# One decoder layer on Trainium2: the low parts of the expert stage's weights, three quarters on GpSimd and one quarter on VectorE, or all on GpSimd

## The reference

```python
qry = (xb @ p['peer_wq']).reshape(PEER_BLOCK, PEER_HEADS, 2, PEER_HALF)
...
top_s, pos = lax.top_k(cand, PEER_TOPK)          # 8 heads x 16 experts a token
idx = jnp.take_along_axis(cidx, pos, axis=-1)
gates = jax.nn.softmax(top_s, axis=-1)
u_rows = p['peer_u'][idx]
act = jax.nn.gelu(jnp.einsum('phkd,pd->phk', u_rows, xb))
coef = gates * act
return jnp.einsum('phk,phkd->pd', coef, p['peer_v'][idx])
```

## Time and profile before

| | us |
|---|---|
| median of 3 runs | 4422.45 |
| the profiled execution, its own time | 4424.48 |
| its span on the core | 4422.7 |
| PE busy in the span | 3754.4 (85%) |
| DVE busy | 3025.6 (68%) |
| POOL busy | 2101.4 (48%) |
| ACT busy | 1477.9 (33%) |
| turns of the expert stage | 2249 to 4399 |

### The profile page before, as it was taken

How to read it: one execution, slowest core, us unless ns; L and a number is a source line. 1 busy time by engine, 2 the same in 40 slices (tenths; PEclk the granted TensorE clock), 3 DMA queues, 4 the chain that set the end, 5 groups by cost and what they waited for, 6 DMA issues and landing times. The chain is left out here.

```text
span 4422.7 us, 65816 instructions
## 1 busy us (share of the span) xinstructions
PE 3754.4 (85%) x24298; PEld 3491.1 (79%) x24298; DVE 3025.6 (68%) x4531; ACT 1477.9 (33%) x1891; POOL 2101.4 (48%) x1162
## 2 busy tenths in 40 slices
PE   6777999999996898987678989988888888888887
PEld 3337888898885797987578988888888888888886
DVE  5777644555554213897967877776778888888886
ACT  5664343443442113223333333232222222222222
POOL 2432222212224133324356767666666667676672
PEclk9998999999997898998889999999999999999998
DMA  8981212222212122223389999999999999999994
GB/s 308 358 314 64 78 64 82 77 77 73 75 67 68 60 98 108 81 70 111 137 315 386 402 395 408 393 384 366 364 381 380 386 401 387 390 395 392 408 403 157
DMA packets 253130, 1090.63 MB, mean 247 GB/s; under 512 B 25352, under 2 KB 78856, under 8 KB 172296
## 3 DMA queue, kind: packets, MB, share of 16 engines
q1 hardware_dynamic: 167440, 543.60, 32.9%
q0 software_dynamic: 73728, 536.90, 29.9%
q10 hardware_dynamic: 11776, 7.52, 0.5%
HBM read 1047.54 MB, written 40.40 MB: 246 GB/s over the span
## 5 line engine op out<-in xcount | busy, mean ns | idle before, releaser
L248 POOL TENSOR_TENSOR wlo<-raw,whi 128x1024 fp32r<-128x1024 f32 x551 | 1343.1, 2441 | 1495.4 <-ACT whi L244 1487.6
L244 ACT CAST whi<-raw 128x1024 fp32r<-128x1024 f32 x672 | 698.8, 1049 | 1284.7 <-DMA raw<-in_u 535.5
L263 PE MATMUL gps<-hi_d,whi 128*128 128x320 f32 x2048 | 661.6, 323 | 168.3 <-POOL wlo L248 116.1
L2096 PE MATMUL gps<-chi,whi 128*128 128x320 f32 x2048 | 653.8, 319 | 124.7 <-DVE outacc L2225 82.0
L263 PE MATMUL gps<-lo_d,whi 128*128 128x320 f32 x2048 | 651.7, 318 | 0.0
L263 PE MATMUL gps<-hi_d,wlo 128*128 128x320 f32 x2048 | 650.6, 318 | 0.0
L2096 PE MATMUL gps<-clo,whi 128*128 128x320 f32 x2048 | 643.2, 314 | 0.0
L2096 PE MATMUL gps<-chi,wlo 128*128 128x320 f32 x2048 | 643.1, 314 | 0.0
L2183 DVE SCALAR_TENSOR_TENSOR dps<-ring,coef,dps 128x2048 f32<-128x2048 f32 x252 | 591.8, 2348 | 7.6 <-DMA ring<-in_v_rows,spi 3.1
L2170 DVE CUSTOM_DVE_ANT_0 ring<-ring,dps 128x2048 f32<-128x2048 f32 x256 | 582.2, 2279 | 0.0
L263 PEld LDWEIGHTS gps<-hi_d,whi 128*128 128x128 f32 x2048 | 402.1, 196 | 186.7 <-POOL wlo L248 126.4
(11 more groups left out here) (388 smaller groups left out, 6064.6 us busy)
## 6 DMA issues: line engine op xcount, KB each, us to landing
raw<-in_u SPq DMA_DIRECT2D x256, 512.0 KB
raw<-in_v SPq DMA_DIRECT2D x256, 512.0 KB
wada<-in_w_ada SPq DMA_DIRECT2D x96, 1024.0 KB, 6.4
raw<-in_w_in SPq DMA_DIRECT2D x96, 512.0 KB
gateD<-gst SPq DMA_DIRECT2D x8, 2560.0 KB, 7.5
gate<-gateD SPq DMA_DIRECT2D x32, 640.0 KB
raw<-in_w_out SPq DMA_DIRECT2D x32, 512.0 KB
raw<-in_w_q SPq DMA_DIRECT2D x32, 512.0 KB
```

The lines of the kernel that those rows point to most:

```text
L244: act.copy(whi[:, k.slot, :], raw_of(k)).then_inc(W.hi, 1)
L248: pool.tensor_tensor(wlo[:, k.slot, :], raw_of(k), whi[:, k.slot, :].bitcast(F32), ALU.subtract).then_inc(W.lo, 1)
L263: m = pe.matmul(gps[:, bank, 0:DT], w, x[:, kt, :], start=(kt == 0 and n == 0), stop=(kt == KT - 1 and n == 2))
L2096: m = pe.matmul(gps[:, 2 + dt, 0:DT], w[:, slot, cols], x[:, buf, c, :], start=(c == 0 and n == 0), stop=(c == NG - 1 and n == 2))
```

## The change

`by_dve` and `split_lo_dve` go, and with them the semaphore `w_lo_dve`. GpSimd makes the low part of every half, in the order of the halves; the 123 that VectorE made are put into GpSimd's stream at their place. Waits for a low part (TensorE's before a half, SyncE's before the load four halves later) are all on one semaphore that counts up by one for each half. Nothing is changed in what TensorE, ScalarE and SyncE do, or in the order in which they do it.

```diff
--- before.py
+++ after.py
@@ -188,7 +188,6 @@
 
         W = Sems()
         W.loaded0, W.loaded1, W.hi, W.lo, W.used = sems(stack, "w_loaded0", "w_loaded1", "w_hi", "w_lo", "w_used")
-        W.lo_dve, = sems(stack, "w_lo_dve")
         w_row = sems(stack, *(f"w_row{n}" for n in range(RING)))
         W.act_steps, W.dve_steps = sems(stack, "w_act_steps", "w_dve_steps")
         act_total, dve_total = [0], [0]
@@ -200,18 +199,9 @@
         N_SHARED = 2 + 12 * H + 2 * KT + 4 * H + 18
         N_DEEP = N_SHARED - 2
 
-        def by_dve(k):
-
-            return k.c >= N_SHARED - 1 and k.slot == 3
-
         def lo_done(k):
 
-            m = k.c - N_SHARED
-            if by_dve(k):
-                return W.lo_dve, m // 4 + 2 + k.i * (k.per // 4)
-            if m < -4 or m < 0 and isinstance(k.n, int):
-                return W.lo, k.n + 1
-            return W.lo, N_SHARED + m // 4 * 3 + m % 4 + 1 + k.i * (k.per // 4 * 3)
+            return W.lo, k.n + 1
 
         def deep(k):
 
@@ -247,11 +237,6 @@
             pool.wait_ge(W.hi, k.n + 1)
             pool.tensor_tensor(wlo[:, k.slot, :], raw_of(k), whi[:, k.slot, :].bitcast(F32),
                                ALU.subtract).then_inc(W.lo, 1)
-
-        def split_lo_dve(dve, k):
-            dve.wait_ge(W.hi, k.n + 1)
-            dve.tensor_tensor(wlo[:, k.slot, :], raw_of(k), whi[:, k.slot, :].bitcast(F32),
-                              ALU.subtract).then_inc(W.lo_dve, 1)
 
         def gemm_dense(pe, k, half, bank):
 
@@ -2035,8 +2020,7 @@
                             fetched[0] += 1
 
                     def lo(k):
-                        if not by_dve(k):
-                            split_lo(pool, k)
+                        split_lo(pool, k)
 
                     def A(g, buf, k, after):
                         for c in range(NG):
@@ -2152,7 +2136,6 @@
                         dve.engine_nop().then_inc(S.acc, 1)
                     for n in range(EARLY * NG):
                         dve.engine_nop().then_inc(S.gel, 1)
-                    dve.engine_nop().then_inc(W.lo_dve, 1)
                     ch = Chain(dve, W.dve_steps, dve_total)
                     taken = [0]
 
@@ -2197,10 +2180,6 @@
                         dve.tensor_tensor(clo[:, buf, c, :], gel, chi[:, buf, c, :].bitcast(F32),
                                           ALU.subtract).then_inc(S.clo, 1)
 
-                    def lo(k):
-                        if by_dve(k):
-                            split_lo_dve(dve, k)
-
                     def A(g, buf, k, after):
                         for c in range(NG):
                             due = rows_due((g - 2) // 2, g % 2 * NG + c)
@@ -2210,8 +2189,6 @@
                             gated(g, c, gps[:, c % 2, 0:DT])
                             take()
                             rest(g, buf, c, gps[:, c % 2, 0:DT])
-                            for j in (2 * c + 2, 2 * c + 3):
-                                lo(k.plus(j) if j < 8 else after.plus(j - 8))
 
                     def B(g, buf, k, after):
                         dve.wait_ge(S.acc, g * KT + 2)
@@ -2223,11 +2200,6 @@
                                     dve.wait_ge(W.used, k.plus(s).n + 1)
                                 out = outacc[:, 2 * s + dt, :]
                                 dve.tensor_tensor(out, out, gps[:, 2 + dt, 0:DT], ALU.add).then_inc(S.acc, 1)
-                                if dt == 0:
-                                    if s < 6:
-                                        lo(k.plus(s + 2))
-                                    elif after is not None:
-                                        lo(after.plus(s - 6))
                             take()
                             if after is None:
                                 if s % 4 == 0:
```

## The result

The kernel became slower. Medians of four runs each on the same chip: 4424.51 us before (4420.88 to 4432.38) and 4476.85 us after (4475.20 to 4490.93), a ratio of 1.0116 (95%: 1.0092 to 1.0139). The forecast was 4400 us with a range up to 4450 us. The profiled execution of the changed kernel took 4490.93 us, 14 us above its median; some of its excess is that run's own, such as the 10 us by which its turns begin later (2259 us, before 2249).

The account below looks back on a forecast made before the run. The prediction took the DMA engines, bringing in gathered rows and weight halves, to bound the expert stage. Its terms, -15 - 5 + 1 - 5 = -24 us on 4424.5 us, gave 4400 us, range 4355 to 4450 us.

Parts of the forecast that it names:

- What bounds the kernel: Expert stage: DMA share 0.98 of 1.02 in both long stretches, so any quicker engine can win at most 76 us.
- VectorE loses 123 low parts: Expert stage: some 190 us leave VectorE; TensorE's removable stalls are 104 us, 31 while u is gathered, 73 while v is.
- How much of that reaches the end: Turns gathering u and v: 5 of 31 and 10 of 73 us are gained, -15 us, bounds 0 and -76.
- The last two Bs: End of the stage, without gathers: TensorE's 3.98 us stop for VectorE's low part goes; -5 us, bounds 0 and -8.
- The first turn: 2249 to 2385 us, DMA not yet full throughout: SyncE no longer waits for VectorE's late part; -5 us, bounds 0 and -6.
- GpSimd's added work: GpSimd gains 123 low parts, 299 us, and is busy 83% and 81% in the long stretches; it keeps up, 0 us.
- Two SBUF readers: Last B: two moved low parts may each stop a small VectorE addition for up to 2 us; +1 us, at most +4.
- DMA alone: Rival: the DMA sets the pace, stalls removed return as load waits, only the end gains; 4419 us, chance 0.22.
- stalls paid in full: Rival: TensorE's removed stalls all count, since earlier high parts start earlier loads and DMA idle patches close; 4342 us, chance 0.08.
- GpSimd becomes the bound: Rival: in As, GpSimd's added parts delay its backlog and later loads; 4453 us, with As of u 4492 us, chance 0.23.
- The signs: Profile after: no TensorE stall for VectorE's low parts, bank waits 78 to 26 us, longer load waits, DMA share 0.98 to 1.0.

Follow-up runs that it names:

- The gates' edit: Gates loaded from ScalarE's queue, one B earlier, instead of SyncE's: kernel before 4345.46 us (0.9807), changed kernel 4338.68 us (0.9798).
- The short parts: Changed kernel, with each of the 123 low parts added to GpSimd covering 128 of 1024 columns: 4484.51 us, 1.0129.
- the edits that moved the lead: Changed kernel, gathers of u issued two rows later: 4441.96 us; also each B's last gather behind the next A's third-half low part: 4421.38 us.
- the idle operations in A and B: Changed kernel, with 123 operations that change nothing where VectorE's low parts stood: 4406.47 us; only those in Bs 4439.08 us, only those in As 4463.66 us.

## Why the prediction was wrong, step by step

- *What bounds the kernel*: right and too coarse. The DMA share of 0.98 was read as "the DMA can't be sped up by more than 76 us", but not as "it can fall". It fell to 0.94. The gates' edit shows that even the ceiling was too low: it made the kernel before 1.9% faster, 88 us on the same chip. The share of 0.98 says how long packets kept the engines, not what they moved: the same rows show 387 and 394 GB/s where the undisturbed stretch had 425, which by the same sum leaves 156 us instead of 76. With the gates moved, the two stretches run at 402 to 414 GB/s.
- *VectorE loses 123 low parts*: right. Waits for them 52 to 0 us, banks 78 to 38 us (26 expected).
- **The step that failed is "How much of that reaches the end"**, with its bounds of 0 and -76 us. I took the worst case as "all given back at the next load". TensorE gave back more than it won: per A of u 5.0 us lost for 2.0 won. The bound of 0 rested on the thought that what the loads wait for is only the full DMA. It is also what stands ahead of them in the queue and among the gathers, and the moment of issue. Both hang on when GpSimd gathers and makes its low parts, and VectorE set that by freeing buffers late (`S.taken`). I had even noted that at an A "everybody waits for the loads queued behind the gates", and used it only to make the gain small.
- *The last two Bs*, -5 us: wrong, -0.3. VectorE's low part ahead of the bank went, and TensorE's stop there went from 3.98 to 2.99 us only. VectorE now stood at a gathered row that had come 0.77 us late:

```profile
4384.70 2.35 DVE L2166 SCALAR_TENSOR_TENSOR ring<-ring,coef,dps 128x2048 f32<-128x2048 f32 x1 [0.77 <-DMA ring<-in_v_rows,spi]
4386.96 0.48 DVE L2180 TENSOR_TENSOR clo<-gps,chi 128x320 fp32r<-128x320 f32 x1
4387.36 0.87 DVE L2202 TENSOR_TENSOR outacc<-outacc,gps 128x320 f32<-128x320 f32 x2
```

  The same row had stood there before (4316.70 us, 2.34 us), ahead of the low part; I had counted the low part as the whole stop.
- *The first turn*, -5 us: wrong. It took 140 us instead of 136, by the same stall (16.6 us of waits for GpSimd's low parts instead of 11.6).
- *GpSimd's added work*, 0 us, 81 to 83% busy: the zero came out on balance, the share is 77 and 78% of a longer stretch. The short parts show both sides: the added time shortens the lead by 1.9 us (u) and 3.2 us (v), and spares the load about as much by holding gathers up. In the sum for the room GpSimd has while u is gathered, 932 us were divided by 116 pairs of halves; seven turns have 112, so a block had 8.3 us, not 8.0.
- *Two SBUF readers*, +1 us: too small to be told apart from nothing.
- *The rivals*: "DMA alone" and "stalls paid in full" were on the wrong side. "GpSimd becomes the bound" had nearly the right time with the As of u in it (4492 us) and the right sign of it, TensorE's waits for GpSimd's low parts growing by more than VectorE's shrink (116 to 258 us, against 52 and 40). But its mechanism, GpSimd working off a backlog after the loads have come, is refuted: the loss would have gone with the short parts. So the near time was luck. Its given argument against ("those waits follow a late load") was the truth about the waits and the wrong reason to leave them out. Its chance of 0.23 didn't cover a second slower way.
- *The signs*: no stalls for VectorE's low parts, GpSimd's waits for VectorE shorter (72 us instead of 240), loads waited for at the start of each A, all seen. The DMA share was to stay between 0.98 and 1.0: 0.94 for u.

What stays open: in which order each DMA engine served its packets; only how much of each queue was moved in the wait is counted. It isn't shown either why GpSimd's low parts and SyncE's issue shifted just as they did, beyond the edits that moved the lead. Also open are how much of the gates' gain is the queue and how much the earlier issue, why the idle operations in A and B are worth more together while v is gathered, and three stops of TensorE of some 9 us for nothing that the profile names (26.2 us before, 28.0 after; a single one of 9.0 to 9.7 us where `LAG` holds and the gates are on SyncE).

## What to carry to other kernels

Where the DMA engines are busy 98% of the time, taking work off another engine need not be worth anything by itself; ask instead what that engine holds back. Work that delays the freeing of a buffer also delays a DMA, and taking it away moves that DMA forward, here into the queue time of the one load that TensorE needs next. Look for the transfer that stands ahead of the critical load in the same queue, and move that (here to another queue, and earlier) before balancing engines: it was worth 2% to either kernel, when the balancing was worth -1.2%.

## What the runs showed of the hardware

- A load of 640 KB took 15.8 to 24.6 us (medians of the runs) from issue to landing on SyncE's queue, shortest in the run with the fewest gathered bytes ahead of the third half (4.4 and 5.9 MB) and longest in the one with the most (6.6 and 8.2), and 32.7 to 34.2 us on ScalarE's, where the kernel was faster. Landing time by itself is no measure of harm.
- Two stretches with nearly the same DMA share, 0.98 and 1.02, moved 387 and 425 GB/s: the share is 4% lower, the rate 9%.
- Making VectorE work 201 us more made a kernel 1.6% faster.
- GpSimd needs 2.42 us for a low part of 1024 columns and 0.47 us for one of 128, and a gather's issue keeps it 0.95 us in the changed kernel, 1.05 us where VectorE is busier.
